# Expert rows weighted and gated as they leave PSUM and scatter-added onto the residual in memory; a transition norm made token-major

## The chip, the cores and the metric

One NeuronCore of a Trainium2 chip runs the whole step in one launch. The metric is the device time of the program in microseconds (us), fp32 throughout.

## The reference

A two-layer backbone over 384 tokens (128 context, 256 latent) of width 1024. Layer 1 mixes tokens with attention, layer 2 with centred window means. Every layer ends in a mixture of 32 experts of which each token takes two. What the change touches is this part, cut from the reference:

```python
for l in range(DEPTH):
    sh1, sc1, g1, sh2, sc2, g2 = ada_modulation(cond, ada_w[l], ada_b[l])
    h = modulate(x, norm_mix_g[l], sh1, sc1)      # rms norm, scale, shift
    ...
        m = multi_scale_pool(h, pool_w[p], pool_scale[p])   # layer 2
    x = x + g1 * m
    h = modulate(x, norm_ffn_g[l], sh2, sc2)
    x = x + g2 * hierarchical_moe(h, ...)
# in hierarchical_moe, combine = the two weights of each token:
hid = silu(a) * b * combine[:, :, None]
y = einsum('tef,efd->td', hid, w_down)
```

`g2` is one vector of 1024 per condition (context or latent), `combine` one number per token and chosen expert.

## The kernel before, in words

Every instruction is placed by hand on its engine's queue and ordered by semaphores. SP loads weights, POOL issues the indirect DMAs, PE multiplies, and ACT and DVE empty PSUM.

**Expert loop (twice, 32 tiles each).** A tile is one expert with up to 64 assigned tokens, and each token's row is held as two half rows of 512, so 128 partitions. Weights come in a ring of four slots (`ring`, 2 MB gate/up, `load_in` L369, and 1 MB down, `load_out` L373) plus a fifth place (`more_gu`, L426). Per tile PE does `gate_up` (L1493, 16 products, 32 records of 256 columns in the trace), `rows_T` of the next tile (L1469), `down` of the tile before (L1517) and `hidden_T` (L1502). A slot is loaded again when its tile's gate/up product (`gu_mm`) and down product (`down_mm`) are over. POOL's `step` issues the gather of the rows of tile s+4 (L516, from `rows` in memory) and the scatter of the result of tile s (L526, to `results` in memory, one row for each assignment). ACT copies the down product from PSUM to one of four `yout` buffers (L782). A buffer's scatter is waited for four tiles later. The rows of a tile beyond its real tokens carry an index out of bounds. An expert with more than 64 tokens gets an extra tile after the loop; layer 1 has one, layer 2 none.

**Layer 1 to layer 2.** When the last scatter has landed (L578, `results_in`), SP loads both result rows of each token (`yrow`, L475). PE multiplies them with diagonal matrices of the weights (L1582), which also turns them channel-major, and DVE gates them and adds them to `xT` (L1142). The mixer norm then takes squares (L713), column sums on PE (L1374), root and reciprocal over 384 columns (L965 to L967), product and modulation (L968 to L973, L723) into `padded`. Window sums follow, two groups on POOL and two on DVE (`pool_group`, L292 to L299), and pooled products (L1605). The weights of the adaLN vectors of layer 2 (`load_ada`, 2 MB each, products at L1194) are woven in.

**End of layer 2.** Results are loaded (L475), ACT scales by the first weight (L811), DVE adds the second and gates (L1169, L1170), POOL or DVE adds the residual (L592, L1173), ACT stores (L817).

## Time and profile before

| what | value |
|---|---|
| median of 3 runs | 941.07 us (939.47 to 941.48) |
| the profiled execution's own time | 938.48 us |
| its span | 936.7 us |
| PE busy | 752.8 us (80%) |
| DVE, POOL, ACT busy | 282.2, 201.9, 187.8 us |
| moved by DMA | 294.9 MB, 315 GB/s over the span |
| chain that ended last | PE 54%, DMA 26%, DVE 11% |

Busy times overlap, so they don't add up to the span. The chain is the sequence of work, each step released by the one before, that ended last. The profiled execution is 0.3% under the median, so a sum made against its time carries over.

### The profile page before, as it was taken

The page shows a single profiled execution, that of the slowest core. Times are in us where ns is not written, and L with a number is a line of the kernel's source. Part 1 is how long each engine was busy: PE and PEld are TensorE (multiplying, and loading weights), DVE is VectorE, ACT ScalarE, POOL GpSimd, SP SyncE. Part 2 cuts the span into 40 slices and gives each one's busy share as a digit, 9 for nine tenths or more (in the row PEclk, how much of TensorE's full clock was granted, in tenths as well). Part 3 has the DMA queues.
Part 4 walks back from the last instruction along what each step waited for, and adds up shares of the span by engine and source line. Part 5 has one row for each costly group of instructions (what it writes and reads, how often), then busy time and mean ns, then how long its engine had stood idle before and what let it go on. Part 6 is the DMA issues. An engine that isn't in the chain of part 4 may idle for free.

```text
span 936.7 us, 12800 instructions
## 1 busy us (share of the span) xinstructions
PE 752.8 (80%) x4603; PEld 414.8 (44%) x4603; DVE 282.2 (30%) x681; ACT 187.8 (20%) x413; POOL 201.9 (22%) x299
## 2 busy tenths in 40 slices
PE   2999977899978997788787749677899988877850
PEld 2544433479344454444444325235455544444420
DVE  0412448731561121111111116855412111111104
ACT  4111155610540111111011104135111110111111
POOL 0000400000013333233332103500233333333112
PEclk9999989999998999999999979687899999999985
DMA  9998700006878999999999979854299999999933
GB/s 355 428 435 313 205 4 11 1 1 269 326 284 341 422 420 419 421 421 421 421 414 393 412 272 376 358 217 135 106 388 410 418 422 424 423 421 423 405 113 153
DMA packets 38614, 294.94 MB, mean 315 GB/s; under 512 B 10584, under 2 KB 11024, under 8 KB 18608
## 3 DMA queue, kind: packets, MB, share of 16 engines
q1 hardware_dynamic: 25328, 273.76, 71.3%
q0 software_dynamic: 11296, 15.09, 5.1%
q10 hardware_dynamic: 1952, 5.58, 1.5%
q8 instruction: 24, 0.39, 0.2%
q14 instruction: 14, 0.11, 0.0%
HBM read 293.84 MB, written 22.02 MB: 337 GB/s over the span
## 4 chain that ended last, share of the span: by engine, by line
PE 54%; DMA 26%; DVE 11%; issue 4%; ACT 2%; POOL 1%; SPq 1%; ACTq 0%; POOLq 0%; DVEq 0%
DMA ring<-in_moe_w_in 19%; PE bank L1493 15%; PE bank L1517 8%; PE bank L1263 7%; PE bank L1359 3%; DMA adaw<-in_ada_w 3%; PE bank L1194 3%; PE bank L1469 2%; DMA adaw<-rows,gcur 2%; PE bank L1374 2%; PE bank L1367 2%; PE bank L1320 2%; PE bank L1388 1%; PE bank L1605 1%; PE bank L1204 1%
## 5 line engine op out<-in xcount | busy, mean ns | idle before, releaser
L1493 PE MATMUL bank<-ring,qkv 128*64 128x256 f32 x2016 | 239.4, 391 | 64.7 <-issue 43.5
L1493 PEld LDWEIGHTS bank<-ring,qkv 128*64 128x64 f32 x2016 | 155.1, 140 | 131.1 <-issue 66.3
L1089 DVE COPY qkv<-bank 128x512 f32<-128x512 f32 x64 | 44.3, 692 | 318.2 <-PE bank L1469 294.1
L526 POOL DMA_INDIRECT results<-adaw,scur x65 | 66.5, 1023 | 286.9 <-ACT adaw L782 258.3
L1517 PE MATMUL bank<-ring,qkv 128*64 128x512 f32 x504 | 122.0, 604 | 1.2 <-DVE qkv L1101 0.8
L516 POOL DMA_INDIRECT adaw<-rows,gcur x65 | 68.0, 1047 | 50.6 <-POOL gcur L513 32.7
L776 ACT ACTIVATE qkv<-bank 128x128 f32<-128x128 f32 x64 | 17.8, 278 | 296.3 <-PE bank L1493 280.2
L782 ACT ACTIVATE adaw<-bank 128x512 f32<-128x512 f32 x64 | 38.2, 597 | 142.7 <-PE bank L1517 140.7
L1263 PE MATMUL bank<-ring,hT 128*128 128x512 f32 x144 | 63.7, 596 | 1.2 <-DVE hT L860 1.2
L1517 PEld LDWEIGHTS bank<-ring,qkv 128*64 128x64 f32 x504 | 31.0, 136 | 47.5 <-issue 45.6
L1469 PE MATMUL bank<-con,adaw 128*128 128x128 f32 x260 | 43.0, 288 | 5.5 <-DMA adaw<-rows,gcur 4.7
L1101 DVE COPY qkv<-bank 128x128 f32<-128x128 f32 x64 | 18.7, 292 | 75.6 <-PE bank L1502 75.6
L1469 PEld LDWEIGHTS bank<-con,adaw 128*128 128x128 f32 x260 | 27.6, 141 | 30.9 <-issue 28.7
L1263 PEld LDWEIGHTS bank<-ring,hT 128*128 128x128 f32 x144 | 26.7, 190 | 32.8 <-issue 31.6
L504 POOL MEMSET adaw<- 128x2048 f32 x2 | 3.6, 1805 | 165.5 <-PE bank L1194 157.7
L1194 PE MATMUL bank<-adaw,condT 128*32 128x512 f32 x176 | 22.8, 639 | 14.3 <-DMA adaw<-in_ada_w 14.3
L1502 PEld LDWEIGHTS bank<-con,qkv 128*128 128x128 f32 x64 | 9.0, 141 | 52.7 <-DVE qkv L1095 51.1
L1194 PE MATMUL bank<-ring,condT 128*32 128x512 f32 x208 | 30.1, 704 | 1.7 <-DMA ring<-in_ada_w 1.7
L1204 PEld LDWEIGHTS bank<-con,adas 128*128 128x128 f32 x176 | 22.1, 197 | 20.5 <-issue 11.2
L672 ACT ACTIVATE ring<-bank,ss 128x384 f32<-128x384 f32 (+1 forms) x48 | 24.0, 506 | 30.5 <-DVE ss L918 30.4
L1359 PE MATMUL bank<-hT,ring 128*128 128x256 f32 x128 | 29.1, 380 | 0.0
L624 ACT ACTIVATE adas<-bank 128x512 f32<-128x512 f32 x24 | 14.3, 596 | 71.0 <-PE bank L1194 71.0
(219 smaller groups left out, 781.3 us busy)
## 6 DMA issues: line engine op xcount, KB each, us to landing
ring<-in_moe_w_in SPq DMA_DIRECT2D x63, 2048.0 KB
ring<-in_moe_w_out SPq DMA_DIRECT2D x63, 1024.0 KB
ring<-in_ada_w SPq DMA_DIRECT2D x13, 2048.0 KB, 12.6
adaw<-in_ada_w SPq DMA_DIRECT2D x11, 2048.0 KB, 12.6
ring<-in_attn_w_qkv SPq DMA_DIRECT2D x3, 2048.0 KB, 35.9
adaw<-results SPq DMA_DIRECT2D x12, 512.0 KB, 6.1
ring<-in_attn_w_o SPq DMA_DIRECT2D x1, 4096.0 KB, 16.7
adaw<-in_moe_w_in SPq DMA_DIRECT2D x2, 2048.0 KB, 14.2
```

The source lines that it names most:

```text
L516: pool.indirect_dma_start(xg[:, b], None, rows, bass.IndirectOffsetOnAxis(ap=gcur[:, b:b + 1], axis=0), bounds_check=row_limit, oob_is_err ...
L526: pool.indirect_dma_start(res, bass.IndirectOffsetOnAxis(ap=scur[:, b:b + 1], axis=0), yout[:, b], None, bounds_check=res_limit, oob_is_er ...
L672: last = A.activation(probs[:, u % 4, j, 0:nk], pairs[u % 2][:, j, 0:nk], ACT.Exp, bias=ss[:, 60 + 2 * (u % 2) + j:61 + 2 * (u % 2) + j], ...
L782: A.activation(yout[:, q], bank[4 + q % 2][:, :], ACT.Copy).then_inc(y_ready, 1)
L1089: V.tensor_copy(xgT[:, p], bank[2][:, :]).then_inc(xgT_ready, 1)
L1194: last = T.matmul(out[32 * j:32 * j + 32, :], condT[:, k, :], w[:, k, :], start=half == 0, stop=half == 1, skip_group_check=True)
L1204: last = T.matmul(bank[2][:, at:at + 2], adas[:, i % 4, j * P:(j + 1) * P], C("sel2"), start=True, stop=True)
L1263: last = T.matmul(bank[5 + g % 3][:, :], hT[:, k, t * P:(t + 1) * P], wqkv[n][:, k, :], start=k == 0, stop=k == KD - 1)
L1359: last = T.matmul(bank[WO_BANKS[d % 2]][:, 0:NTOK - CTX], wo[:, k, d * P:(d + 1) * P], hT[:, k, CTX:NTOK], start=k == 0, stop=k == KD - 1)
L1469: last = T.transpose(bank[2][:, i * P:(i + 1) * P], xg[:, q, i * P:(i + 1) * P], ident)
L1493: last = T.matmul(bank[p][64 * a:64 * a + 64, 0:2 * P], xk[:, k % 4, k // 4], w[:, :, k, a * P:(a + 1) * P], start=k == 0, stop=k == KD - ...
L1517: last = T.matmul(bank[4 + p][64 * a:64 * a + 64, :], hidT[:, p, 64 * j:64 * j + 64], w[j][:, a * 512:(a + 1) * 512], start=j == 0, stop=j ...
```

## The change

1. **Results.** DVE takes over from ACT: for each tile it copies the tile's weight and a context flag (`wcur`), builds the gate row (`gdiff` times flag plus `glat`) and multiplies the down product from PSUM with weight and gate. `yout` has two buffers. POOL scatters with `compute_op=ALU.add`: in layer 1 onto `x_dram`, in layer 2 straight onto the outputs, with two DMAs per tile (prompt rows, sample rows; the other's rows are out of bounds).
2. **Order of the scatters.** Before its scatter of tile s POOL waits for that of tile s-1.
3. **Residual.** Ahead of the experts the residual is turned token-major (`keep`, 6 groups of 4 transposes, 6 copies, 3 stores) in both layers. The table of assignments gets a second product for the weights, and `gate_rows` (16 products) and two DVE operations spread the gate vectors once a layer.
4. **Transition.** SP loads `x_dram` back (3 x 512 KB). Each token tile gets its sum of squares on ACT, a diagonal of reciprocals on DVE, and products with the diagonal that turn and normalise it at once; ACT and DVE write one half each into `padded`. The combine, the norm's column sums and the 384-column reciprocal are gone. Pooling differences are made in place in `padded`, and the pooled products are split by segment (32 products in place of 16, same columns).
5. **Adjacent.** adaLN loads and products of layer 2 are spread differently (six loads behind the x tiles, the others behind the window sums). `rcount` and `poolw` are loaded by SP after tile 8's weights.
6. **End.** There is nothing behind the last scatter of layer 2.

Core of the diff:

```diff
@@ POOL @@
-                def scatter(s, b, copied, n, result, m, arrived):
-                    G.tensor_copy(scur[:, b:b + 1], sidx[:, bass.ds(s, 1)]).then_inc(copied, 1)
+                def scatter(s, p, copied, n, result, m, arrived):
+                    G.tensor_copy(scur[:, p, :], sidx[:, bass.ds(s, 1), :].rearrange("p a c -> p (a c)")).then_inc(copied, 1)
                     pool.wait_ge(copied, n + 1)
                     pool.wait_ge(result, m)
-                    pool.reg_alu(res_limit, res_limit, 0, ALU.max)
-                    pool.indirect_dma_start(
-                        res, bass.IndirectOffsetOnAxis(ap=scur[:, b:b + 1], axis=0),
-                        yout[:, b], None, bounds_check=res_limit, oob_is_err=False).then_inc(arrived, 16)
+                    for i, (rows_of, limit) in enumerate(targets):
+                        pool.reg_alu(limit, limit, 0, ALU.max)
+                        pool.indirect_dma_start(
+                            rows_of, bass.IndirectOffsetOnAxis(ap=scur[:, p, i:i + 1], axis=0),
+                            yout[:, p], None, bounds_check=limit, oob_is_err=False,
+                            compute_op=ALU.add).then_inc(arrived, 16)
...
                     if old:
-                        pool.wait_ge(s_y[b], s * 4 + (16 * users(l, b, NBUF) - 4 * b))
-                    scatter(s, b, pool_order, n, y_ready, l * NE + s + 1, s_y[b])
+                        pool.wait_ge(s_y[(b + 1) % 2], scattered(l, s + 1, (b + 1) % 2))
+                    else:
+                        pool.wait_ge(s_xout, l * 48 + 48)
+                        pool.wait_ge(idx_ready, l * 2 + 2)
+                    scatter(s, b % 2, pool_order, n, y_ready, l * NE + s + 1, s_y[b % 2])
@@ DVE @@
+                def result(s, p, old=True):
+                    dve.wait_ge(down_mm, l * NE + s + 1)
+                    if old:
+                        dve.wait_ge(s_y[p], scattered(l, s, p))
+                    V.tensor_copy(wcur[:, p, :], wm[:, bass.ds(s, 1), :].rearrange("p a c -> p (a c)")).then_inc(y_order, 1)
+                    dve.wait_ge(y_order, s * 2 + (l * NE * 2 + 1))
+                    V.scalar_tensor_tensor(yout[:, p], gdiff, wcur[:, p, 1:2], glat, ALU.mult, ALU.add).then_inc(y_order, 1)
+                    dve.wait_ge(y_order, s * 2 + (l * NE * 2 + 2))
+                    V.scalar_tensor_tensor(yout[:, p], bank[4 + p][:, :], wcur[:, p, 0:1], yout[:, p], ALU.mult, ALU.mult)\
+                        .then_inc(y_ready, 1)
@@ SP @@
-                sp.wait_ge(results_in, l + 1)
-                for t in range(TT):
-                    ...
-                    for k in range(2):
-                        sp.dma_start(yrow[:, t, k], res_dram[l][k * NTOK + t * P:k * NTOK + (t + 1) * P, :])\
-                          .then_inc(s_yrow[t], 16)
+                    sp.wait_ge(results_in, 1)
+                    for t in TILES_BACK:
+                        sp.dma_start(xtok[:, t, :], x_dram[0][t * P:(t + 1) * P, :]).then_inc(s_xin[t], 16)
@@ PE @@
+                    for n, t in enumerate(TILES_BACK):
+                        pe.wait_ge(dg_ready, n + 1)
+                        for q in range(2):
...
+                                last = T.matmul(bank[3 + 2 * (n % 2) + q][:, k * P:(k + 1) * P],
+                                                xtok[:, t, (4 * q + k) * P:(4 * q + k + 1) * P], dg[:, t], start=True, stop=True)
-                                last = T.matmul(bank[4 + n % 2][:, k * P:(k + 1) * P],
-                                                yrow[:, t, c2, (4 * q + k) * P:(4 * q + k + 1) * P], diag[:, 2 * t + c2],
-                                                start=c2 == 0, stop=c2 == 1)
-                    norm_pe(1)
```

`scattered(l, s, p)` is the count that stands when all earlier scatters of that buffer have landed: for POOL's wait ahead of tile s it is reached with the landing of tile s-1, for DVE's with that of tile s-2.

How the instructions stand. POOL, one step in the loop of layer 2 (gather, then scatter; `adaw` is the memory that holds `xg` and `yout`), before:

```order
L513 COPY gcur<-gidx 128x1
L514 REGISTER_ALU
L515 REGISTER_ALU [waits pool_order]
L516 DMA adaw<-rows,gcur 128x512
L537 ISA
L522 REGISTER_ALU [waits s_y1]
L522 COPY scur<-sidx 128x1
L523 REGISTER_ALU
L525 REGISTER_ALU [waits y_ready,pool_order]
L526 DMA results<-adaw,scur 1536x512
```

and now:

```order
L528 COPY gcur<-gidx 128x1
L529 REGISTER_ALU
L530 REGISTER_ALU [waits pool_order]
L531 DMA adaw<-rows,gcur 128x512
L554 ISA
L537 ISA [waits s_y0]
L537 COPY scur<-sidx 128x2
L538 REGISTER_ALU
L541 REGISTER_ALU [waits y_ready,pool_order]
L542 DMA out<-adaw,scur 256x512
L541 REGISTER_ALU
L542 DMA out<-adaw,scur 512x512
```

A step has one indirect DMA more. The wait on a landed scatter (`s_y`) stands at the same place, but there are two such semaphores in turn where there were four.

DVE in the expert loop (L1089 rows, L1095 hidden product, L1101 turned hidden), before:

```order
L1088 REGISTER_ALU [waits xg_mm]
L1089 COPY qkv<-bank 128x512 [waits gu_mm]
L1092 REGISTER_ALU
L1094 REGISTER_ALU [waits silu_ready]
L1095 TENSOR_TENSOR qkv<-bank,qkv 128x128 [waits hid_mm]
L1101 COPY qkv<-bank 128x128 [waits down_mm,hid_mm]
```

and now:

```order
L1120 COPY qkv<-bank 128x512 [waits gu_mm]
L1123 REGISTER_ALU
L1125 REGISTER_ALU [waits silu_ready]
L1126 TENSOR_TENSOR qkv<-bank,qkv 128x128 [waits hid_mm]
L1132 COPY qkv<-bank 128x128 [waits down_mm,hid_mm]
L1138 ISA [waits down_mm]
L1139 ISA [waits s_y1]
L1139 COPY wcur<-wm 128x2
L1140 REGISTER_ALU
L1141 SCALAR_TENSOR_TENSOR adaw<-qkv,wcur 128x512 [waits y_order]
L1142 REGISTER_ALU
L1143 SCALAR_TENSOR_TENSOR adaw<-bank,wcur,adaw 128x512 [waits y_order]
```

The three operations of `result` follow in the same queue, behind a wait for `down_mm` and one for a landed scatter, so the next tile's row copy stands behind both.

DVE at the transition, before:

```order
L1142 SCALAR_TENSOR_TENSOR xT<-bank,mods,xT 128x128 [waits mix_mm1]
L1142 SCALAR_TENSOR_TENSOR xT<-bank,mods,xT 128x128 x3
L965 TENSOR_SCALAR qkv<-bank 128x384 [waits st_mm,pad_zero]
L967 RECIPROCAL qkv<-qkv 128x384 [waits std_ready]
L968 TENSOR_TENSOR hT<-xT,qkv 128x384 [waits dve_order]
L971 TENSOR_TENSOR hT<-xT,qkv 128x384
L973 TENSOR_SCALAR adaw<-hT,mods 128x128 [waits xr_ready]
...
L292 TENSOR_TENSOR qkv<-adaw 128x2x415 [waits s_pool,h_ctx,h_new]
```

and now:

```order
L1204 RECIPROCAL ss<-ss 128x1 [waits std_t]
L1205 TENSOR_SCALAR dg<-con,ss 128x128 [waits dve_order]
...
L1214 TENSOR_SCALAR adaw<-bank,mods 128x128 [waits pad_zero,nt_mm]
L1214 TENSOR_SCALAR adaw<-bank,mods 128x128 x3
L1204 RECIPROCAL ss<-ss 128x1 [waits std_t]
L1205 TENSOR_SCALAR dg<-con,ss 128x128 [waits dve_order]
...
L293 TENSOR_TENSOR qkv<-adaw 128x2x415 [waits s_pool,h_ctx]
```

The window sums (L292, now L293) stood behind the gated adds and a norm over all 384 columns; they now stand behind three diagonals and three groups of four evictions.

## Rows read from the trace of the kernel before

**Rows 1.** The page: GB/s in 40 equal slices of the span.

```profile
GB/s 355 428 435 313 205 4 11 1 1 269 326 284 341 422 420 419 421 421 421 421 414 393 412 272 376 358 217 135 106 388 410 418 422 424 423 421 423 405 113 153
```

**Rows 2.** Windows: us, busy by engine (x instructions), PEclk, DMA share, GB/s.

```profile
283.60:356.00 72.40, 69.32 (x487) 35.94 (x487) 12.96 (x33) 8.86 (x21) 26.94 (x44) 0.98 1.00 406
356.00:519.50 163.50, 129.51 (x902) 73.40 (x903) 23.64 (x61) 17.66 (x41) 48.48 (x79) 0.99 1.00 416
...
546.70:588.00 41.30, 32.84 (x228) 20.27 (x229) 20.74 (x43) 12.43 (x23) 11.28 (x8) 0.88 0.86 343
588.00:606.00 18.00, 11.60 (x62) 4.09 (x61) 17.38 (x21) 2.26 (x4) 9.32 (x6) 0.66 0.84 339
606.00:625.00 19.00, 18.87 (x48) 9.74 (x48) 5.94 (x16) 4.19 (x8) 0.00 (x0) 0.87 0.78 332
625.00:667.70 42.70, 30.10 (x118) 18.04 (x117) 28.03 (x94) 17.83 (x26) 3.24 (x6) 0.72 0.24 78
...
749.00:903.00 154.00, 126.55 (x858) 68.28 (x859) 22.12 (x57) 17.22 (x39) 43.35 (x71) 0.97 0.94 392
```

**Rows 3.** Timeline of POOL, one step of layer 1: start us, us, engine, line.

```profile
454.09 1.02 POOL L526 DMA_INDIRECT results<-adaw,scur  x1 [4.84 <-ACT adaw L782]
...
456.09 1.05 POOL L516 DMA_INDIRECT adaw<-rows,gcur  x1 [0.78 <-POOL gcur L513]
...
462.18 1.03 POOL L526 DMA_INDIRECT results<-adaw,scur  x1 [4.84 <-ACT adaw L782]
```

**Rows 4.** Timeline of PE in layer 1: two gate/up products, one after a stall.

```profile
324.03 3.67 PE L1493 MATMUL bank<-ring,qkv 128*64 128x256 f32 x32
...
330.35 0.87 PE L1493 MATMUL bank<-ring,qkv 128*64 128x256 f32 x6
...
470.80 5.36 PE L1493 MATMUL bank<-ring,qkv 128*64 128x256 f32 x32 [1.88 <-issue]
```

**Rows 5.** Timeline of POOL where layer 1's last scatters are waited for.

```profile
528.93 0.98 POOL L526 DMA_INDIRECT results<-adaw,scur  x1 [1.40 <-ACT adaw L782]
536.93 0.18 POOL L522 COPY scur<-sidx 128x1 uint32<-128x1 uint32 x1 [7.03 <-DMA results<-adaw,scur]
538.98 0.99 POOL L526 DMA_INDIRECT results<-adaw,scur  x1 [1.86 <-ACT adaw L805]
546.66 0.10 POOL L578 MEMSET scur<- 128x1 uint32 x1 [6.69 <-DMA results<-adaw,scur]
```

**Rows 6.** Timeline of POOL at the end of layer 2.

```profile
905.37 0.99 POOL L526 DMA_INDIRECT results<-adaw,scur  x1 [1.40 <-ACT adaw L782]
908.65 0.10 POOL L578 MEMSET scur<- 128x1 uint32 x1 [2.29 <-DMA results<-adaw,scur]
```

**Rows 7.** DMA issues: line, engine, count, KB each, median us to landing.

```profile
adaw<-results SPq DMA_DIRECT2D x12, 512.0 KB, 6.1
...
out<-xtok ACTq DMA_DIRECT2D x3, 512.0 KB, 2.6
adaw<-rows,gcur POOLq DMA_INDIRECT x65, 8.6
results<-adaw,scur POOLq DMA_INDIRECT x65, 7.4
```

**Rows 8.** Timeline: first scatter of layer 1; first product and scatter of layer 2.

```profile
298.25 1.05 POOL L526 DMA_INDIRECT results<-adaw,scur  x1 [8.41 <-ACT adaw L782]
...
667.74 3.22 PEld L1493 LDWEIGHTS bank<-ring,qkv 128*64 128x64 f32 x32 [1.18 <-DVE qkv L1089]
...
680.88 1.03 POOL L526 DMA_INDIRECT results<-adaw,scur  x1 [8.48 <-ACT adaw L782]
```

**Rows 9.** Timeline: DVE's first window sum; ACT's scaling; the last store.

```profile
587.94 1.01 DVE L292 TENSOR_TENSOR qkv<-adaw 128x830 f32<-128x830 f32 x1
...
913.66 1.15 ACT L811 ACTIVATE adaw<-adaw,wts 128x1024 f32<-128x1024 f32 x1 [9.12 <-DMA adaw<-results]
...
927.99 0.34 ACTq L817 DMA_DIRECT2D out<-xtok  x1
```

More of the change, by code:

```diff
@@ L58 @@
 _n = 0
-for _name, _w in (("ident", P), ("ones", P), ("upper", P), ("sel2", 2), ("rep", 2 * P), ("assign", 6),
+for _name, _w in (("ident", P), ("ones", P), ("upper", P), ("sel2", 2), ("assign", 6), ("eps", 1),
                   ("half", 1), ("place", P), ("tiles", NT), ("first", NE), ("rev", NE), ("revg", NG), ("extra", EXTRA),
@@ L82, in constants @@
     put("sel2", (p % 32) == np.arange(2)[None, :])
-    put("rep", np.concatenate([np.repeat((p % 32) == j, P, 1) for j in range(2)], 1))
-    put("assign", np.concatenate([k * NTOK + t * P + p for k in range(2) for t in range(TT)], 1) - NONE)
+    put("eps", EPS)
+    put("assign", np.concatenate([t * P + p for k in range(2) for t in range(TT)], 1) - NONE)
     put("half", 2 * NONE + p // TC)
@@ L294, in pool_group @@
             for first, at, m in SEGS:
-                out = hT[:, 2 * g:2 * g + 2, first:first + m]
                 a = at - WINDOWS[g] // 2
-                order(E.tensor_tensor(out, src[:, :, a:a + m],
+                total, own = src[:, :, a:a + m], padded[:, 2 * g:2 * g + 2, at:at + m]
+                order(E.tensor_tensor(total, total,
                                       rcount[:, g, first:first + m].unsqueeze(1).to_broadcast([P, 2, m]), ALU.mult))
-                last = E.tensor_tensor(out, out, padded[:, 2 * g:2 * g + 2, at:at + m], ALU.subtract)
+                last = E.tensor_tensor(own, total, own, ALU.subtract)
                 if first == 0:
@@ L565, in _ @@
                             gather(NE, 0, x_idx[l], 0, xs_g[l])
-                for b in range(NBUF):
-                    pool.wait_ge(s_y[b], 16 * users(l + 1, b, NBUF))
+                for p in range(2):
+                    pool.wait_ge(s_y[p], scattered(l, NE + p, p))
                 def extra(j):
@@ L1109, in experts @@
                 hidden_T(1, 1, old=False)
+                result(0, 0, old=False)
                 loops = (NE - 3) // 2
@@ L1446, in _, with gate_rows @@
                 last.then_inc(tab_mm, 1)
+                keep(2)
+                keep(3)
                 if l == 0:
-                    ada(BETWEEN - 1)
-                    ada_vectors(BETWEEN - 2)
-                    ada_vectors(BETWEEN - 1)
-                if l == 1:
-                    pe.wait_ge(x_down[1], 1)
-                    for n in range(4):
-                        if n >= 2:
-                            pe.wait_ge(g2_ready, n - 1)
-                        T.matmul(bank[6 + n % 2][:, :], C("rep")[:, (n // 2) * P:(n // 2 + 1) * P],
-                                 adas[:, (2 * NCH - 2 + n % 2) % 4, :], start=True, stop=True).then_inc(g2_mm, 1)
-                pe.wait_ge(idx_ready, l * 2 + 2)
+                    ada(LATE + 4)
+                    ada_vectors(LATE + 3)
+                else:
+                    ada_vectors(BETWEEN + 7)
+                keep(4)
+                keep(5)
+                if l == 0:
+                    ada(LATE + 5)
+                    ada_vectors(LATE + 4)
+                    ada_vectors(LATE + 5)
+                pe.wait_ge(slots_ready, l * 12 + 12)
+                for i in range(6):
+                    last = T.matmul(bank[6][:, 0:NT], at_place[:, i], in_tile[:, i], start=i == 0, stop=i == 5)
+                last.then_inc(tab_mm, 1)
+                def gate_rows():
+                    for b, cond in ((7, 1), (6, 0)):
+                        for a in range(2):
+                            for j in range(4):
+                                last = T.matmul(bank[b][64 * a:64 * a + 64, j * P:(j + 1) * P],
+                                                mod(l, 5, 4 * a + j, cond).to_broadcast([P, 64]), ident,
+                                                start=True, stop=True, skip_group_check=True)
+                    last.then_inc(gates_mm, 1)
                 def rows_T(s, q, old=True):
@@ L1541, in _ @@
                 hidden_T(0, 0, old=False)
+                gate_rows()
+                pe.wait_ge(x1_copied, l * 6 + 6)
                 first = RING + 2
@@ new lines, in _ @@
+                    for n in range(6):
+                        t, q = TILES_BACK[n // 2], n % 2
+                        if n == 1:
+                            pe.wait_ge(h_new, KD + 2)
+                        if n >= 2:
+                            pe.wait_ge(xt_copied, 6 + n - 1)
+                        for k in range(4):
+                            last = T.transpose(bank[RAW_BANKS[n % 2]][:, k * P:(k + 1) * P],
+                                               xtok[:, t, (4 * q + k) * P:(4 * q + k + 1) * P], ident)
+                        last.then_inc(xt_mm, 1)
@@ L1640 @@
     args += [nc.dram_tensor(f"out_{i}", s, F32, kind="ExternalOutput").ap() for i, s in enumerate(_OUTS)]
-    args += [[nc.dram_tensor(f"{n}{l}", s, F32, kind="Internal").ap() for l in range(2)]
-             for n, s in (("rows", (NTOK, D)), ("results", (2 * NTOK, D)))]
+    args += [[nc.dram_tensor(f"{n}{l}", (NTOK, D), F32, kind="Internal").ap() for l in range(m)] for n, m in (("rows", 2), ("x", 1))]
     build(nc, *args)
```

431 lines of the change are left out of this document (243 added, 188 removed).

## The prediction

> **What bounds the kernel now.** I read the slices first, then windows cut where the stages change, then the POOL timeline, because the change moves work onto POOL's scatters. In the slices the two expert loops show as the long flat stretches at 420 GB/s, with a dip between them and one at the end [rows 1]. The windows say the same with engines [rows 2]. In the first 72 us of loop 1 PE is busy 69 us; from 356 to 519.5 PE has 34 us free while the DMA share is 1.00. So the loops are bound by weights: PE runs ahead on five preloaded experts at 6.32 us a tile (330.35 - 324.03) [rows 4], then tiles come every 8.09 us (462.18 - 454.09) [rows 3]. Behind them lie 121 us from the landing of layer 1's last result (546.66) to layer 2's first product (667.74) [rows 5, 8], and 31.3 us from the last scatter's issue (905.37) to the end of the span.
>
> The trace has no accumulating scatter, but it has what one must wait for. The issue list gives 7.4 us from a scatter's issue to its landing [rows 7]. With weights queued, the scatter of 528.93 frees POOL at 536.93 (8.0 us) and that of 538.98 at 546.66 (7.7 us) [rows 5]. With idle queues the one of 905.37 frees it at 908.65 (3.3 us) [rows 6]. Today this costs nothing in the loop, since POOL waits for a landing four tiles late. Now tile s waits for tile s-1.
>
> **Terms.** All against the profiled execution (span 936.7, own time 938.48, so 1.8 us around it; 0.3% under the median).
>
> *Scatter chain, the largest term.* From landing to next issue: a 0.2 us index copy, a wait for it, the issue. The same pair for a gather takes 0.97 us from copy to DMA (456.09 - 455.12, the copy ends 0.78 before the DMA starts) [rows 3]. So one link under load is 8.0 + 1.0 = 9.0 us, and 3.3 + 1.0 = 4.3 idle. In layer 2 a second DMA is issued behind the first, 1.0 us on POOL [rows 3], and its landing ends the wait: 10.0 and 5.3 us. Is it loaded? A tile's 3 MB take some 7.5 us at 420 GB/s [rows 1], and SP issues them when the down product is over, about 2 us ahead of that tile's scatter. So yes, for nearly the whole link. Both links exceed 8.09, so the chain sets the pace and DVE's wait for tile s-2 passes it back to PE. For the price of adding in memory there is no row: nothing is the lower end (with the 3.1 MB more that each layer reads, 7.4 us, inside the wait), one more landing phase under load as the upper, 7.4 - 3.3 = 4 us a DMA. I take 0, nearest to the plain scatter's row, and keep the other for the range.
>
> *Layer 1.* Scatter 0 was at 298.25 [rows 8]. Add 3 us for six groups of transposes and the second table product on PE ahead of the loop, and 1 us since DVE's three operations replace one ACT copy: 302. The last three links are unloaded, because the weights for layer 2 are then in: 302 + 28 x 9.0 + 3 x 4.3 = 567. The extra tile now comes strictly behind: landing 3.3, DVE and index 3, landing 3.3, so 576, against 546.66: **+29**.
>
> *Transition.* Tiles of 512 KB land in 3 to 6 us (2.6 and 6.1 in the issue list) [rows 7]; a square takes about 1.15 us (that of ACT at 913.66) [rows 9], a diagonal, products and evictions some 3 us, pipelined over three tiles: window sums start 13 us after the landing; before, it was 41.3 (587.94 - 546.66) [rows 5, 9]. Sums 17 (window 588 to 606 [rows 2]). Half of the pooled products no longer wait for the last sum, so 11 in place of 19 (606 to 625). Two adaLN products moved in behind the norm cost 5, the router to first product stays 42.7 - 0.7 = 42 (window behind 625). 13 + 17 + 11 + 5 + 42 = 88 for 121: **-33**. Bounds: -15 if the tiles don't overlap and the adaLN loads come late, -40 if they don't show. The six loads queue behind the x tiles on SP, 5 us each, hidden by the sums; so are `keep` and `gate_rows`, by weights already in flight.
>
> *Layer 2.* First product at 576 + 88 = 664. Scatter 0 stood 13.1 us behind it (680.88 - 667.74) [rows 8], now 15.5: 679.5. Weights are all in after tile 25 or so, then the longer of the idle link and PE's 6.4 binds: 679.5 + 25 x 10.0 + 6 x 6.5 = 968.5. That is 304.5 us behind the first product, against 237.6 (905.37 - 667.74): **+67**.
>
> *End.* Gone are results in, scaling, gating and adding. Before, the last store's issue (927.99) came 8.7 us ahead of the end with a landing of 2.6 [rows 7, 9], so 6.1 remain behind a landing. Now 968.5 + 4.3 + 6.1 = 979: the end costs 10.4 in place of 31.3, **-21**.
>
> *Costed at nothing:* `result` on DVE, some 1.7 us a tile on an engine 14% busy in the loop (window 356 to 519.5 [rows 2]); if it weren't hidden, 1.7 x 63 = 107 us. ACT is relieved and gains nothing, being off the path.
>
> Sum: 938.5 + 29 - 33 + 67 - 21 = 980.5; the walk through the times gives 979 + 1.8 = 981. I say **980 us**, 39 above the median.
>
> **Against the skill.** The trace's landing is 7.4 us loaded, 3.3 idle [rows 6, 7]. The Trainium skill, DMA: Bandwidth & Descriptors, section on the anatomy of one DMA, fits 2.0 us plus bytes over 436 GB/s: at 256 KB that would be an estimate of 2.6 us, a link of under 5 us, and the chain would hide. By that the time is rival A's. The loaded row speaks against it, the idle row nearly for it.
>
> **Rivals.**
>
> *A. The chain hides (faster).* A scatter slips between weight packets once queues are less deep than before. Both loops are then weight-bound: the last scatter of layer 1 at 528.93 + 3 + 7.4 = 539, extra tile under load 19 more, 558; plus 88 is 646; layer 2's loop 237.6 + 7.4 us, end 10.4: 901.6, so **903 us**. For it: the idle landing. Against: loads of 7.5 us leave only 0.6 us of 8.09 idle.
>
> *B. The chain binds, but at the weights' pace.* The landing shortens as far as the idle share allows: links 8.2 and 9.0. 28 x 0.8 + 25 x 1.0 = 47 less: **933 us**. The mean link at which the change turns from loss to gain is about 8.7 us.
>
> *C. Adding in memory costs.* Two more us a DMA, half the upper end: links 11 and 13 or so, 28 x 2 + 25 x 3 = 131 more: **1110 us**. For: every row is read, added, written. Against: no row.
>
> *D. PE falls to the lower clock.* After a stall of 1.88 us one gate/up product took 5.36 us where others take 3.67 [rows 4]. Stalls grow to about 3 us a tile. A tile of 8.0 still fits in 9.0 and costs nothing; all of it at half rate (1.2 GHz) is 12.6 us and would bind, 28 x 3.6 + 25 x 2.6 = 166 more, 1146. I give it little, as PE was busy 79% at a granted clock of 0.99 in the bound stretch [rows 2].
>
> *E. The transition isn't shorter* (a load late): 998, inside the range.
>
> **Chances.** Forecast with its spread (links 8.5 to 10, transition -15 to -40) 0.62; A 0.14; B 0.10; C 0.11; D 0.03. Within 0.2% of before is about what a measurement of this kernel can tell from no change. Faster: A, B, 0.24; same 0.04, from the forecast's edge; slower 0.72. Range 905 to 1065: it leaves out the lower half of A, C and D, together some 0.2.
>
> **What would show it.** POOL's waits: indirect scatter copies waiting on their own DMA, some 60 times, 5 to 8 us each (right), or next to none (A). Scatters 9 us apart in layer 1 and 10 in layer 2. DMA share under 1 in both loops, about 0.9 and 0.85. Landing to first window sum 13 us, landing to first product 88. Last landing to end 6 us. I am wrong if scatters stand 8.1 us apart or less, if landing takes under 6 us in the loop, or if DVE or PE is what the chain names there.

## The result, and the profile after

The changed kernel takes **1051.4 us** (median of four runs, 1036.9 to 1056.7) against 940.6 us for the kernel before beside it: slower, ratio 1.107, 95% interval 1.102 to 1.112. The two longer of the four count as a slower state, so that the ratio and every difference from the changed kernel below are taken from the other two, whose middle is 1042.2 us; with runs that far apart, some 10 us are no result. The forecast was 980. Direction and cause were right, the size was not: about 39 us were forecast above the kernel before, 102 came (111 by the median of all four). The profiled execution is one of the longer ones (span 1053.4, own time 1055.3), so the pieces below add up to some 13 us too much; kernels below that differ from it by a detail have spans of 1040 to 1046 and the same pattern of links.

Time was lost in three places and won in two:

| piece, us | before | after | difference | forecast |
|---|---|---|---|---|
| start of the span to first scatter of layer 1 | 298.25 | 312.79 | +14.5 | +4 |
| first scatter to landing of the extra tile | 248.4 | 297.5 | +49.1 | +25 |
| that landing to layer 2's first product | 121.1 | 96.7 | -24.4 | -33 |
| first product to the last tile's scatter | 237.6 | 334.9 | +97.2 | +67 |
| that scatter to the end | 31.3 | 11.5 | -19.8 | -21 |

The page of the kernel after, in slices. The two plateaus at 420 GB/s of [rows 1] are gone:

```profile
PEclk9799989999689888889889679959898877888885
...
GB/s 361 428 406 217 129 1 11 1 240 333 267 303 401 359 360 318 343 356 378 369 362 316 148 311 312 318 255 285 287 271 356 294 316 306 262 361 293 307 103 15
```

The windows of the kernel after, columns as in [rows 2]: scatters of layer 1, the transition, layer 2's first 27 links, its last four.

```profile
312.79:596.57 283.78, 217.71 (x1342) 104.48 (x1340) 86.92 (x183) 8.31 (x30) 90.97 (x118) 0.86 0.91 349
610.30:706.99 96.69, 77.12 (x466) 51.59 (x466) 58.59 (x157) 38.39 (x69) 23.68 (x25) 0.82 0.83 324
726.21:1015.75 289.54, 204.29 (x1248) 98.16 (x1246) 78.33 (x168) 7.76 (x28) 125.70 (x135) 0.83 0.80 303
1015.75:1041.85 26.10, 12.70 (x86) 5.78 (x82) 7.43 (x15) 0.55 (x2) 13.21 (x12) 0.81 0.16 18
```

In neither loop is any engine or the DMA full. What each waits for, from the list of waits (us in total, times, longest):

```profile
POOL scur L537 <- DMA x<-adaw,scur: 147.9, 32, 7.2
PE bank L1556 <- DMA adaw<-rows,gcur: 138.1, 30, 9.2
...
POOL scur L537 <- DMA out<-adaw,scur: 118.7, 27, 8.9
...
DVE wcur L1139 <- DMA out<-adaw,scur: 101.2, 18, 10.8
DVE wcur L1139 <- DMA x<-adaw,scur: 90.9, 25, 7.6
```

POOL waits 59 times for its own scatter, as often as forecast ("some 60 times, 5 to 8 us each"), though for 4.5 us on average (266.6 / 59), where in the loop before it waited for ACT. The chain that ended last, by engine, is below; of its 37% of DMA the landings of `x<-adaw,scur` are 19% and those of `out<-adaw,scur` 13%:

```profile
DMA 37%; PE 29%; issue 15%; DVE 8%; POOL 7%; ACT 2%; POOLq 1%; ACTq 0%; DVEq 0%
```

Two links of layer 1, timeline of POOL (compare [rows 3, 5]): the copy of the index starts when the scatter before has landed.

```profile
353.00 1.59 POOL L542 DMA_INDIRECT x<-adaw,scur  x1 [0.80 <-POOL scur L537]
354.05 0.75 POOL L528 COPY gcur<-gidx 128x1 uint32 x1
355.57 1.06 POOL L531 DMA_INDIRECT adaw<-rows,gcur  x1 [0.77 <-POOL gcur L528]
360.30 0.19 POOL L537 COPY scur<-sidx 128x2 uint32 x1 [3.67 <-DMA x<-adaw,scur]
361.29 1.60 POOL L542 DMA_INDIRECT x<-adaw,scur  x1 [0.80 <-POOL scur L537]
...
372.12 0.19 POOL L537 COPY scur<-sidx 128x2 uint32 x1 [7.19 <-DMA x<-adaw,scur]
373.11 1.60 POOL L542 DMA_INDIRECT x<-adaw,scur  x1 [0.80 <-POOL scur L537]
```

Issue to landing is 7.3 us in one (353.00 to 360.30), 10.8 in the next (361.29 to 372.12), so the links are 8.3 and 11.8 long. And layer 2, with two DMAs a tile, timeline of POOL and then PE:

```profile
810.57 1.59 POOL L542 DMA_INDIRECT out<-adaw,scur  x1 [0.80 <-POOL scur L537]
812.47 1.55 POOL L542 DMA_INDIRECT out<-adaw,scur  x1 [0.30 <-issue]
...
824.66 0.18 POOL L537 COPY scur<-sidx 128x2 uint32 x1 [8.52 <-DMA out<-adaw,scur]
825.63 1.59 POOL L542 DMA_INDIRECT out<-adaw,scur  x1 [0.79 <-POOL scur L537]
827.52 1.55 POOL L542 DMA_INDIRECT out<-adaw,scur  x1 [0.30 <-PE bank L1556]
...
831.20 0.20 POOL L537 COPY scur<-sidx 128x2 uint32 x1
```

```profile
813.42 3.67 PE L1580 MATMUL bank<-ring,qkv 128*64 128x256 f32 x32
826.24 1.12 PE L1556 MATMUL bank<-con,adaw 128*128 128x128 f32 x4 [9.15 <-DMA adaw<-rows,gcur]
827.29 3.64 PE L1604 MATMUL bank<-ring,qkv 128*64 128x512 f32 x8
```

Long and short links alternate: 15.1 us (810.57 to 825.63), then 6.6, in which POOL finds the landing already there. A down product takes 1.94 us at 803.82, two tiles earlier; here, behind 9.15 us without work, it takes 3.64. The granted clock was 1.00 over the first and 0.52 from 826.24 to 830.93: the upper and the lower of its two levels.

### The profile page after: what moved, and what is told of

Its sections match the earlier page's. It is cut to its first block, busy times and chain, and to the rows that moved or that the text cites. A ratio compares the mean times of both kernels' runs of the same rounds, so it can differ in the third digit from the quotient of the medians.

```text
span 1053.4 us, 13425 instructions
## 1 busy us (share of the span) xinstructions
PE 805.6 (76%) x4715; PEld 430.5 (41%) x4715; DVE 367.6 (35%) x862; ACT 152.0 (14%) x362; POOL 281.1 (27%) x328
## 3 DMA queue, kind: packets, MB, share of 16 engines
q0 software_dynamic: 19648, 13.31, 6.9%
## 4 chain that ended last, share of the span: by engine, by line
DMA 37%; PE 29%; issue 15%; DVE 8%; POOL 7%; ACT 2%; POOLq 1%; ACTq 0%; DVEq 0%
DMA x<-adaw,scur 19%; DMA out<-adaw,scur 13%; PE bank L1325 6%; DMA adaw<-rows,gcur 4%; POOL out L542 4%; PE bank L1256 3%; PE bank L1421 3%; PE bank L1580 2%; PE bank L1266 2%; PE bank L1429 1%; PE bank L1382 1%; PE bank L1455 1%; PE bank L1436 1%; DVE qkv L293 1%; POOL scur L537 1%
## 5 line engine op out<-in xcount | busy, mean ns | idle before, releaser
L1556 PE MATMUL bank<-con,adaw 128*128 128x128 f32 x260 | 53.4, 340 | 152.4 <-DMA adaw<-rows,gcur 138.1
L1604 PE MATMUL bank<-ring,qkv 128*64 128x512 f32 x504 | 157.0, 755 | 1.2 <-DVE qkv L1132 0.8
L542 POOL DMA_INDIRECT out<-adaw,scur x64 | 101.3, 1584 | 52.9 <-POOL scur L537 23.7
L1556 PEld LDWEIGHTS bank<-con,adaw 128*128 128x128 f32 x260 | 34.2, 168 | 179.4 <-DMA adaw<-rows,gcur 149.4
L537 POOL COPY scur<-sidx 128x2 uint32 (+1 forms) x65 | 12.0, 185 | 266.9 <-DMA x<-adaw,scur 147.9
L1139 DVE COPY wcur<-wm 128x2 f32 (+1 forms) x64 | 10.8, 169 | 192.1 <-DMA out<-adaw,scur 101.2
L542 POOL DMA_INDIRECT x<-adaw,scur x33 | 52.8, 1601 | 46.3 <-POOL scur L537 23.6
L528 POOL COPY gcur<-gidx 128x1 uint32 (+1 forms) x65 | 44.0, 677 | 45.7 <-DVE gidx L1094 43.7
L514 POOL MEMSET adaw<- 128x2048 f32 x2 | 3.6, 1806 | 174.7 <-PE bank L1256 166.0
L1141 DVE SCALAR_TENSOR_TENSOR adaw<-qkv,wcur 128x512 f32<-128x512 f32 x64 | 48.2, 753 | 2.3
L1143 DVE SCALAR_TENSOR_TENSOR adaw<-bank,wcur,adaw 128x512 f32<-128x512 f32 x64 | 48.1, 751 | 2.3
## 6 DMA issues: line engine op xcount, KB each, us to landing
adaw<-in_ada_w SPq DMA_DIRECT2D x12, 2048.0 KB, 10.8
```

What stands on the lines that cost most here:

```text
L528: G.tensor_copy(gcur[:, b:b + 1], gidx[:, bass.ds(s, 1)]).then_inc(copied, 1)
L542: pool.indirect_dma_start(rows_of, bass.IndirectOffsetOnAxis(ap=scur[:, p, i:i + 1], axis=0), yout[:, p], None, bounds_check=limit, oob_is ...
L1141: V.scalar_tensor_tensor(yout[:, p], gdiff, wcur[:, p, 1:2], glat, ALU.mult, ALU.add).then_inc(y_order, 1)
L1143: V.scalar_tensor_tensor(yout[:, p], bank[4 + p][:, :], wcur[:, p, 0:1], yout[:, p], ALU.mult, ALU.mult)\
L1556: last = T.transpose(bank[2][:, i * P:(i + 1) * P], xg[:, q, i * P:(i + 1) * P], ident)
L1604: last = T.matmul(bank[4 + p][64 * a:64 * a + 64, :], hidT[:, p, 64 * j:64 * j + 64], w[j][:, a * 512:(a + 1) * 512], start=j == 0, stop=j ...
```

## The experiments

Times are medians, each in the same session as runs of the kernel before (941 to 943 us). "Link" is the mean time from one tile's scatter to the next, over 31 links. In the kernel before links are 7.44 us in layer 1 and 7.24 in layer 2; in the changed one 9.15 and 10.18 (its profiled run being a long one; e2, e5 and e12, near it in all, have 9.07 to 9.19 and 9.97 to 10.08).

| run | edit | us | ratio, 95% | links |
|---|---|---|---|---|
| e1 | before, plain scatters in a serial chain | 979.6 | 1.039-1.045 | 8.52, 7.82 |
| e2 | changed, index copied ahead of the wait | 1053.3 | 1.117-1.124 | 9.19, 9.97 |
| e3 | changed, no adding | 977.0 | 1.031-1.041 | 8.32, 8.54 |
| e4 | changed, one DMA a tile in layer 2 | 1013.8 | 1.071-1.080 | 9.12, 8.91 |
| e5 | changed, four row buffers | 1045.5 | 1.107-1.113 | 9.07, 10.02 |
| e6 | changed, gather behind scatter | 1072.1 | 1.130-1.139 | 9.51, 10.62 |
| e7 | e4 and e5, two targets in turn | 930.6 | 0.986-0.989 | 7.80, 7.56 |
| e8 | plain, four in flight, rest as changed | 926.7 | 0.976-0.988 | 7.38, 7.23 |
| e9 | changed, nearly no weights loaded | 886.4 | 0.939-0.945 | 6.61, 7.04 |
| e10 | e8, residual kept inside the loop | 923.4 | 0.978-0.983 | 7.38, 7.27 |
| e11 | changed, index copied twice | 1076.6 | 1.138-1.147 | 9.53, 10.66 |
| e12 | e5, gathers one tile earlier | 1047.1 | 1.100-1.114 | 9.15, 10.08 |

**e1: the chain alone.** In the kernel before:

```
-    pool.wait_ge(s_y[b], s * 4 + (16 * users(l, b, NBUF) - 4 * b))
+    c = (b - 1) % NBUF
+    pool.wait_ge(s_y[c], s * 4 + (12 + 16 * users(l, c, NBUF) - 4 * c))
```

> The kernel before, with one edit: POOL waits for the landing of scatter s-1, not of s-4, ahead of scatter s. Nothing is added in memory, one DMA a tile, evictions on ACT as before. Theory (the serial chain of landings sets the pace): links of 8.0 + 1.0 = 9.0 us in both layers, last scatter less first scatter 265 us in each in place of 231 and 225, together about 75 more, so some 1010 us. Rival (adding in memory, or the second DMA, makes the links long; a plain scatter in a chain hides): scatters stay 8.1 us apart and the time within 10 us of 940. Rival (DVE's wait and its three operations set the pace): also near 940, since they are not here.

39 us slower, by the wait alone, with no adding, no second DMA and the evictions still on ACT. That is the forecast's chain, at half its price: links of 8.5 where 9.0 was put, and in layer 2 a tail of links of 3 to 5 us, where nothing is loaded any more. Its loop, in windows of the two layers:

```profile
301.33:565.53 264.20, 217.72 (x1399) 104.61 (x1399) 36.08 (x92) 27.72 (x63) 72.05 (x118) 0.92 0.95 386
701.56:922.00 220.44, 188.68 (x1221) 92.73 (x1219) 31.86 (x81) 23.65 (x54) 63.37 (x103) 0.91 0.97 394
```

**e3: the adding.** `compute_op=ALU.add` taken out of the changed kernel's scatter.

> The changed kernel with plain scatters in place of accumulating ones, waits and everything else as they are. It leaves out the addition in memory, so a row holds the last thing written. Theory (adding costs only its issue on POOL: 1.60 us against 1.02): 0.6 us a DMA, 32 + 64 DMAs, 58 us less, links of 8.6 and 9.5, about 990. Rival (adding also lengthens the landing, each row being read and written): links come down to 8.1 in layer 1, and the time falls by 90 or more, to 955 or lower. Rival (adding costs nothing that counts): under 15 us less.

65 us less than the changed kernel, between the theory's 58 and the rival's 90. Adding costs 0.8 us a link in layer 1 (9.15 - 8.32) and 1.6 in layer 2 (two DMAs; 1.4 to 1.5 against e2 and e5). Its issue on POOL is 1.60 us against 1.02, the median from issue to landing in layer 1 is 8.5 us against 7.7, and it puts more packets in the queue. The software queue's line of the page, of the changed kernel and of e3 (packets, MB, share of 16 engines' time):

```profile
q0 software_dynamic: 19648, 13.31, 6.9%
```

```profile
q0 software_dynamic: 13440, 13.28, 4.6%
```

With adding gone, 36 us are left over the kernel before. That this is near e1's 39 is chance, since e3 still has the change's other pieces: from first to last scatter its two loops are 67 us longer than before (258 and 265 us), e1's 51, with one DMA a tile; the start adds 13 to e3, transition and end give back 24 and 19.

**e4: the second DMA.**

```
-    targets = ((y_prompt[0].rearrange("t (a n) -> (t a) n", a=2), prompt_limit),
-               (y_sample[0].rearrange("t (a n) -> (t a) n", a=2), sample_limit))
+    targets = ((x_dram[0].rearrange("t (a n) -> (t a) n", a=2), row_limit),)
```

> The changed kernel with one accumulating DMA a tile in layer 2 also, into the residual in memory in place of the two outputs. It leaves out layer 2's expert sums in the outputs. Layer 1 is untouched. Theory (the second DMA adds its issue, 1.9 us from first to second, to every link): layer 2's links go from 10.7 to about 9.0 us under load, 45 to 60 us less, about 995. Rival (the second DMA's issue hides in the landing of the first, behind the weights in the queues): under 15 us less, layer 2's span from first to last scatter stays over 300 us.

28 us less, and layer 2's link 8.91 in place of 10.18: 1.27 us (1.1 against e2 and e5), not the 1.9 between the two issues. Part of the second issue hides in the first's landing.

**e2 and e11: POOL's own part of the link.** e2 moves the index copy ahead of the wait; e11 does it twice:

```
-    G.tensor_copy(scur[:, p, :], sidx[:, bass.ds(s, 1), :].rearrange("p a c -> p (a c)")).then_inc(copied, 1)
-    pool.wait_ge(copied, n + 1)
+    for i in range(2):
+        G.tensor_copy(scur[:, p, :], sidx[:, bass.ds(s, 1), :].rearrange("p a c -> p (a c)")).then_inc(copied, 1)
+        pool.wait_ge(copied, n + 1 + i)
```

> The changed kernel, with the copy of scatter s's index moved ahead of the wait for scatter s-1's landing; all else as it is. Theory (POOL's serial link is landing, index copy, wait for the copy, issue): each link loses the copy and the wait behind it, 0.97 us, 60 times: 45 to 60 us less, about 990 against 1045. Rival (the landing stretches to fill what the weights leave, so that the pace is set by the DMA queues): under 15 us less. Rival (DVE, which waits for the same landing with its two buffers and then works 1.7 us, sets the pace): under 10 us less, and POOL is then seen waiting for DVE's result.

> The changed kernel with the copy of the scatter's index, and the wait behind it, done twice between the landing of scatter s-1 and the issue of scatter s: e2's edit with the sign turned. Theory (the landing is elastic: a scatter lands when the weights in the queues with it have landed, so that time taken from or added to POOL's part comes back in the landing): under 15 us more, the landing's share of POOL's wait shorter by what was added. Rival (POOL's part adds in full, and e2 failed for another reason): 0.97 us a link, 60 us more, about 1105.

Neither theory holds in full. Taking 0.97 us out of every link gives nothing (1053, among the changed kernel's own runs of 1037 to 1057). The second copy puts in 0.86, not 0.97 (from landing to issue 1.85 us for 0.99), and costs 34 us, about half a microsecond a link. So a link is not landing plus copy plus issue, as the forecast summed it. The short links show one reason: POOL doesn't wait in them, it works (index copies, two scatters, a gather) for 6.6 us, and e2 leaves that work as long as it was. In the long ones the landing gave back what was taken: the two links of layer 1 above are 8.0 and 11.8 us long in e2, and its landings take just that, for 7.3 and 10.8. Why the landing stretches so, and why e11's addition cost only a part of itself, is left open.

**e5, e12, e6: who holds whom.** e5 gives the weighted rows four buffers, e12 adds gathers a tile earlier, e6 sets the gather behind the scatter:

```
-    yout = cc[:, 2048:3072].rearrange("p (b n) -> p b n", b=2)
+    yout = cc[:, 2048:4096].rearrange("p (b n) -> p b n", b=4)
...
-    dve.wait_ge(s_y[p], scattered(l, s, p))
+    dve.wait_ge(s_y[p], scattered(l, s, p) - 16 * (l + 1))
```

```
-    pool.wait_ge(xg_mm, l * NE + s + 1)
-    gather(s + NBUF, b, pool_order, n, s_xg[b])
+    pool.wait_ge(xg_mm, l * NE + s + 2)
+    gather(s + 1 + NBUF, (b + 1) % NBUF, pool_order, n, s_xg[(b + 1) % NBUF])
```

> The changed kernel with four buffers for the weighted rows in place of two, so that DVE waits for the landing of scatter s-4, not of s-2; POOL's chain stays serial and accumulating. Theory (coupling: the landing that holds DVE holds PE's next products, so the loads of two tiles are issued in one burst behind a landing and the next scatter queues behind them; that is why taking 1 us out of POOL's link gave nothing): the alternation of short and long links (7 and 14 us in layer 2) fades, the DMA share of layer 2's loop rises from 0.74 to 0.85 or more, its mean link falls from 10.2 to about 9, layer 1's from 9.15 to about 8.8: 40 to 50 us less, about 1000. Rival (POOL's serial chain alone sets the pace, however many buffers DVE has): links and time as they are, within 15 us of 1045.

> The kernel of e5 (four buffers for the weighted rows), with each gather issued one tile earlier in POOL's order, as soon as the rows of tile s+1 have been transposed. Theory (PE's 138 us of waits for gathers are lockstep: POOL, held by a landing, issues the gather late, it lands behind a burst of weights, PE restarts late and at the lower clock, and only then are the next loads issued): PE's waits for gathers fall under 50 us, the bursts even out, layer 2's links fall from 10.0 to about 9, 30 to 50 us less than e5's 1045. Rival (the waits for gathers are only back pressure of a chain that is bound by itself): PE's waits move to another place, and the time stays within 10 us of 1045.

> The changed kernel with the gather of tile s+4 issued behind scatter s instead of ahead of it, all waits the same. Theory (coupling, bursts of weights): the gather's 256 KB are no large part of what a scatter queues behind, under 15 us either way. Rival (gather and scatter share one queue, and the gather ahead of each scatter is what lengthens its landing): up to 0.6 us a link, and the wait of POOL for the gather's index goes off the chain, 1.9 us a link in all: 60 to 100 us less. Rival (gathers are late: the profile names them for 138 us of PE's waits): issued a link later they hold PE more, 30 us or more slower.

I had come to think that DVE's wait for a landing, and the late gathers, made the bursts. e5 and e12 speak against it: within 5 us of the changed kernel, with links as before. DVE's waits for scatters in the loop are gone from e5's list, but not POOL's, and not PE's for gathers:

```profile
PEld bank L1563 <- DMA adaw<-rows,gcur: 153.1, 31, 11.7
POOL scur L538 <- DMA x<-adaw,scur: 144.7, 32, 7.2
PE bank L1563 <- DMA adaw<-rows,gcur: 139.5, 32, 10.8
POOL scur L538 <- DMA out<-adaw,scur: 113.6, 28, 9.3
```

With gathers a tile earlier (e12) PE still waits 141.4 us for them. I take these waits for back pressure: with more room PE runs ahead and then stands. No run shows that by itself. Gathers do count when they come later still (e6, 30 us more, as its last rival had it), and taking them from ahead of the scatter, in the queue they share, gained nothing.

**e9: the weights.** Loads of 64 columns in place of whole experts, all else the same.

> The changed kernel, every wait and instruction as it is, but each load of an expert's weights behind the first five moves 64 of its columns alone (96 KB a tile in place of 3 MB). It leaves out most of the expert weights. Theory (the chain is long because each scatter and gather lies in the queues behind weights; the adding by itself is short): POOL waits 2 us or less for a landing, links fall to 6.3 to 6.6 us, the pace of PE, in both layers: about 31 x 2.7 + 31 x 3.6 = 195 less, some 850. Rival (an accumulating scatter is slow by itself, 7 us or more from issue to landing whatever else moves): links stay at 9 or more, and the time near 1045.

Timeline of POOL in layer 1, and in layer 2:

```profile
414.21 1.60 POOL L544 DMA_INDIRECT x<-adaw,scur  x1 [2.31 <-DVE adaw L1145]
415.27 0.75 POOL L530 COPY gcur<-gidx 128x1 uint32 x1
416.79 1.07 POOL L533 DMA_INDIRECT adaw<-rows,gcur  x1 [0.77 <-POOL gcur L530]
418.11 0.75 POOL L539 COPY scur<-sidx 128x2 uint32 x1 [0.26 <-DMA x<-adaw,scur]
```

```profile
756.30 1.59 POOL L544 DMA_INDIRECT out<-adaw,scur  x1 [0.80 <-POOL scur L539]
758.19 1.55 POOL L544 DMA_INDIRECT out<-adaw,scur  x1 [0.30 <-PE bank L1558]
759.17 0.77 POOL L530 COPY gcur<-gidx 128x1 uint32 x1
760.76 1.10 POOL L533 DMA_INDIRECT adaw<-rows,gcur  x1 [0.82 <-POOL gcur L530]
762.19 0.18 POOL L539 COPY scur<-sidx 128x2 uint32 x1 [0.33 <-DMA out<-adaw,scur]
763.16 1.59 POOL L544 DMA_INDIRECT out<-adaw,scur  x1 [0.79 <-POOL scur L539]
```

The same serial, accumulating chain, 156 us faster. In layer 1 a scatter issued at 414.21 has landed by 418.11, 3.9 us, and POOL then waits for DVE: links of 6.3, PE's pace. In layer 2 POOL waits for little but its own copies: its sequence takes 6.86 us a tile (756.30 to 763.16), just over PE's 6.3. An accumulating scatter is short alone (median issue to landing 3.7 us in layer 1 of e9) and 8.5 among weights. The time, 886, is 36 above the figure expected. Layer 2's links are POOL's (7.04 where 6.6 at most was put, some 14 us in all), layer 1 has two of 11 to 12 us near its end, where layer 2's first experts are loaded in full, and layer 2 has an extra tile here, 8.1 us behind the last scatter (865.88 to 874.02), presumably since layer 1's incomplete sums send other tokens to its experts.

**e7: two in flight.** Four buffers and one DMA a tile as above, and tile s waits for tile s-2, since the two add into different tensors:

```
+    rows_of = x_dram[b % 2].rearrange("t (a n) -> (t a) n", a=2)
...
-    pool.wait_ge(s_y[(b + 1) % 2], scattered(l, s + 1, (b + 1) % 2))
+    pool.wait_ge(s_y[b % 2], scattered(l, s, b % 2))
```

> Four buffers as in e5, one accumulating DMA a tile as in e4, and even and odd tiles add into two different tensors, so that a scatter waits for the one two tiles back. It leaves out the sums of the odd tiles in layer 1 and all of layer 2's in the outputs. Against e4 (1014 us). Theory (the serial wait is what makes an accumulating scatter cost): with two in flight both loops are bound by weights, 8.1 us a tile, first to last scatter some 240 in layer 1 and 230 in layer 2 in place of 283 and 276: about 925. Rival (the adding itself loads the DMA queues, so depth doesn't help): links stay near 9, 985 to 1015.

930.6: 83 us under e4, which differs only in buffers (these alone, e5, gave nothing) and in the two targets with the depth of two that they allow. Every scatter still adds, and the loops are bound by weights again:

```profile
305.39:541.00 235.61, 201.32 (x1330) 110.57 (x1326) 83.28 (x180) 8.33 (x30) 89.39 (x116) 0.95 1.00 399
679.99:911.00 231.01, 200.26 (x1330) 106.11 (x1326) 82.80 (x179) 8.33 (x30) 88.50 (x114) 0.95 0.96 381
```

The Trainium skill, DMA: Bandwidth & Descriptors, section Rules for kernel authors, says that a write which lands between an accumulating DMA's read and write of the same bytes is lost, and to wait for the earlier DMA's semaphore. No run here tried that; e7 keeps the rule by giving the two scatters different bytes.

**e8: a version that beats both.** Plain scatters as before the change, into a tensor of results with a row for each choice, four in flight; weighting and gating on DVE, the residual kept on the chip, the token-major norm as changed.

```
-            rows_of, bass.IndirectOffsetOnAxis(ap=scur[:, p, i:i + 1], axis=0),
-            yout[:, p], None, bounds_check=limit, oob_is_err=False,
-            compute_op=ALU.add).then_inc(arrived, 16)
+        res, bass.IndirectOffsetOnAxis(ap=scur[:, b:b + 1], axis=0),
+        yout[:, b], None, bounds_check=res_limit, oob_is_err=False).then_inc(arrived, 16)
...
+    for k in range(2):
+        V.tensor_tensor(xtok[:, t, :], xtok[:, t, :], yslot[2 * n + k], ALU.add)
```

> Computes all of it. The changed kernel with plain scatters into a tensor of results with a row for each choice, four in flight, as in the kernel before; rows are still weighted and gated on DVE, the residual stays on the chip, and DVE adds two rows a token onto it between the layers and at the end; the norm stays token-major. Theory (adding in memory and its serial chain are the whole loss of the loops, DVE's 1.7 us a tile hides): loops as before the change, 240 and 225 us from first to last scatter; start 12 us later than before; transition 97 + 5 for twice the loads = 102 in place of 121; end 22 in place of 31: 938 + 12 - 19 - 9 = 922. Rival (DVE's three operations a tile are on the path once the chain is gone): loops 20 to 50 us longer each way, 950 to 1000.

926.7 us, 1.8% under the kernel before (1.2 to 2.4%). Layer 1 runs from 309.29 to 538.08, 228.8 us, and layer 2 from 674.59 to 898.86, 224.3, where the kernel before has 230.7 and 224.5. So DVE's three operations don't set the pace. They aren't free: the first scatter stands 19.0 and 18.9 us behind its layer's first product where it stood 14.6 and 13.1, and from first product to last scatter the loops are 2.5 and 5.5 us longer than before (some 1.8 of the last is the first gate/up product, 5.49 us for 3.67). Transition: 554.34 to 655.69, 101.3, with 102 expected. End: 24.3 against 31.3. Windows of both loops:

```profile
309.29:536.00 226.71, 192.78 (x1330) 105.36 (x1326) 83.33 (x181) 8.32 (x30) 71.46 (x117) 0.98 1.00 415
674.59:896.00 221.41, 195.65 (x1330) 103.45 (x1326) 82.77 (x179) 8.31 (x30) 70.03 (x114) 0.97 0.96 397
```

**e10: the late start.** In e8, the six groups of transposes go into steps 3 to 5 of the loop:

```
     for s in range(1, first):
         step(s, s % NBUF, old=s - 1)
+        if s >= 3:
+            keep(2 * s - 6)
+            keep(2 * s - 5)
```

> Computes all of it. The kernel of e8 (plain scatters, four in flight), with the six groups of transposes that keep the residual token-major moved from ahead of the expert loop into its steps 3 to 5, so that layer 1's last adaLN products stand where they stood before the change. Theory (the groups ahead of the loop hold up the adaLN products on which POOL's clearing of the gather buffers and so the first gather waits, 281 against some 275 us; in the loop they hide behind weights): first product of layer 1 at 284 to 286 in place of 290.3, and the same again, 2 to 4 us, in layer 2: about 917 against 926.7. Rival (the start is bound by the second table product and the weights, or PE's 1.3 us a step more in the loop costs as much as it gives): within 3 us of 926.7.

923.4, the best of all; its interval and e8's overlap, so the 3 us between them aren't shown by the time. POOL's clearing of the gather buffers waits for an adaLN product. It starts at 272.82 in the kernel before, at 284.40 in the changed one, 281.12 in e8 and here at

```profile
277.40 1.80 POOL L519 MEMSET adaw<- 128x2048 f32 x1 [158.91 <-PE bank L1272]
...
282.13 0.18 POOL L529 COPY gcur<-gidx 128x1 uint32<-128x1 uint32 x1 [2.93 <-DVE gidx L1093]
```

and layer 1's first product follows at 288.17 (290.27 in e8). These times also hold what differs from one execution to the next ahead of that wait: with the groups ahead of the loop the clearing starts at 281.1 to 284.6, but at 277.3 in e7. The wait itself, the figure in the bracket, is cleaner. It is 157.7 us in the kernel before, 159.0 in e1, 158.9 here, and 163.1 to 166.6 in all eleven runs with the groups ahead of the loop. So the groups held it, by 4 to 9 us. 4.5 us of the start are still there, 3.4 of them from ahead of that wait.

## Why the prediction was right, and where it failed

**What bounds the kernel after: right.** The serial chain of landings costs the time: e1 makes it of the kernel before with one wait, e7 takes it away with all the adding left in.

**Adding in memory, put at nothing: the step that failed.** "I take 0, nearest to the plain scatter's row" is the error. It measured 0.8 us a link in layer 1 and 1.6 in layer 2, and 65 of the 102 us go when it is taken out (e3). Of it 0.58 us a DMA is issue on POOL. Rival C had the mechanism with 2 us a DMA and 1110 us; the truth lies between it and the forecast.

**Scatter chain, links of 9.0 and 10.0: too high for what they described.** The sum was landing plus copy plus issue, 8.0 + 1.0, and 1.0 for a second DMA. The plain chain runs at 8.5 in layer 1 (e1), where a plain scatter lands in 7.2 us (median) and not in 8.0. (The 7.4 of [rows 7] is one landing: its least, middle and greatest are the same figure, while e1's run from 2.1 to 12.6.) With two plain DMAs a tile layer 2's mean link is 8.54 (e3), 9.3 forecast. So this error hid part of the other: layer 1's mean link was 9.15 with 8.55 forecast (28 of 9.0, 3 of 4.3), layer 2's 10.18 with 9.3 (25 of 10.0, 6 of 6.5). That e3's 977 us meets the forecast's 980, which also has adding at nothing, is luck: piece by piece e3 is +13, +23, -24, +47 and -19 where +4, +25, -33, +67 and -21 were put. Layer 2's loop was put 20 us too long, start and transition together 18 too short.

**Unloaded links at the ends: half right.** Layer 2's last four take 6.5 us, as put, at a DMA share of 0.16. But they begin two links later than put, and in layer 1 links stay loaded to the end (9.5, 9.9, 9.4 ahead of the last), since layer 2's first two experts are loaded there. The extra tile took 13.7 us from the last scatter (596.57 to 606.34, landing 610.30) for 9 forecast.

**Start, +4: wrong, +14.5.** I costed transposes and a table product by their own time and did not follow the adaLN products behind them on PE to POOL's clearing, the gathers and the first product (293.18 for 283.64). e10 shows that path: 8.3 us came in POOL's wait ahead of the clearing (166.0 for 157.7). Another 3.0 came behind the clearing. The last 3.3 were there before that wait began, over a first 100 us with a granted clock of 0.93 for 1.00; with the changed kernel's code there that wait begins anywhere from 114.2 to 118.6 us in the runs, so I don't count them as the change's price.

**Transition, -33: right in sign, -24.4.** Landing to first window sum 16.1 us (610.30 to 626.40) for 13; to first product 96.7 for 88. Where the other 5.6 us lie wasn't taken apart.

**First scatter of layer 2: put too early.** It was put 15.5 us behind the first product and stood 19.2 behind it (706.99 to 726.21), which is in the +97.2.

**End, -21: right, -19.8.** The last DMA is issued at 1043.71, 9.7 ahead of the end; 3.7 of landing (e9's median) and 6 behind it.

**`result` on DVE, nothing: right to a few us.** e8 shows it with the chain gone: links as long as before, and 2.5 and 5.5 us a layer by the later first scatter.

**Rivals.** A (the chain hides) is out: it hides in neither e1 nor e3. By the Trainium skill's fit (DMA: Bandwidth & Descriptors, anatomy of one DMA) 256 KB would take an estimated 2.6 us. The idle landings are the ones near it, 3.3 us plain [rows 6] and 3.7 adding (median in layer 1 of e9); among weights the trace says 8.5. B (933) is out: it had links of 8.2 in layer 1, under even e1's 8.5. D is out: the granted clock fell to 0.86 and 0.83 in the loops and single products ran at half speed, but behind waits, and PE is busy only 204 of 290 us in layer 2's loop. E's share of the loss is 9 us.

**Range.** 1042 and 1051 lie inside 905 to 1065, because the range reached toward C, not because the sum came near.

## What to carry to other kernels

A scatter that adds to rows which the one before may touch was made to wait for its landing here, and a landing costs what the queues hold: 3.7 us alone, 8.5 behind weights. Ask how many may be in flight before asking what one costs. Plain rows and an addition later (e8) kept 20 of the 24 us won at the transition and 7 of the 20 at the end. Two targets in turn (e7) brought the loops back to the weights' pace, but e7 leaves out adding the two targets together, and no run has the price of that. And price a stretch ahead of a loop by what stands behind it on the same engine, not by its own time.

## What the runs showed that I had not expected

- Adding in memory lengthens the issue: 1.60 us on POOL for 1.02, and the software queue's packets rise from 13440 to 19648 at the same 13.3 MB.
- A link is elastic: 0.97 us taken from it gave nothing, 0.86 added cost about 0.5.
- With a serial, accumulating chain links alternate, between 7 and 11.5 us in layer 1 and between 6.7 and 15 in layer 2; neither more buffers (e5) nor earlier gathers (e12) evened them. The plain chain of e1 hardly alternates: 7.6 to 9.4 us from the second link of layer 1 to the 26th. What sets the pairs was not found.
- The same code ahead of the loop brought POOL to its clearing of the gather buffers anywhere from 277.3 to 284.6 us: a few us at the start of one profile are no finding.
